# A hybrid SSM and attention block in one kernel: query/key/value projected among the convolution's tiles, z and the gates as half tiles inside the scan and attention

## The reference, cut to what matters

```python
h = rms_norm(x, norm_mix_w)
P = h @ w_in                     # columns [z | xBC | dt | q | k | v | gate_ssm | gate_attn]
u = silu(causal_dwconv(xBC))     # width 4, over 4096 channels
y, state = ssd_scan(xs, softplus(dt + b), -exp(a_log), B, C)   # chunks of 128 tokens; 8 per sample sequence
y = (y + xs * d_skip) * silu(z)
y = y * rsqrt(mean over each of 8 groups (y * y) + eps) * ssm_norm_w
A = y @ w_ssm_out
B = sliding_window_attention(rope(q), rope(k), v, sinks) @ w_attn_out
x = x + (sigmoid(gate_ssm) * A + sigmoid(gate_attn) * B) @ w_out
x = x + peer(rms_norm(x))        # retrieval among 16384 experts, then a final norm
```

## Time and profile before

| | |
|---|---|
| median of 3 runs | 2969.11 us (2968.07 to 2972.53) |
| profiled execution | 2970.44 us around a span of 2968.6 us |
| mean granted clock of TensorE | 0.931 |
| busy share: PE, DVE, ACT, POOL | 93%, 64%, 31%, 23% |
| split on ScalarE (L1021) | 373 x 1.06 us |
| split on GpSimd (L488) | 213 x 2.53 us |

### The profile page before, as it was taken

One profiled execution on the slowest core, in us unless ns is written; L12 is line 12 of the kernel. 1 busy time (PEld: TensorE's weight loads), 2 busy tenths in 40 slices (PEclk: granted clock), 3 DMA queues, 4 the chain that ended last, 5 costly groups with the idle time before them and its releaser, 6 DMA issues.

```text
span 2968.6 us, 46810 instructions
## 1 busy us (share of the span) xinstructions
PE 2768.2 (93%) x15762; PEld 2406.5 (81%) x15762; DVE 1888.6 (64%) x3749; ACT 915.0 (31%) x1527; POOL 683.4 (23%) x345
## 2 busy tenths in 40 slices
PE   6997789997779999989999999999998999999997
PEld 5996668995369999988888888887887888888886
DVE  5998874325620582227799998884667777755554
ACT  2333440044412441123333345553221211211211
POOL 1332000021003324323345423333441111100000
PEclk9998885588869999999999999999999999999999
DMA  3221002321002212312334335457999888866662
GB/s 120 78 78 62 1 0 101 117 96 50 1 27 85 78 64 78 108 66 93 113 132 146 141 149 197 179 191 278 335 342 292 290 289 289 274 196 193 190 196 83
DMA packets 253899, 430.31 MB, mean 145 GB/s; under 512 B 146912, under 2 KB 149600, under 8 KB 252384
## 3 DMA queue, kind: packets, MB, share of 16 engines
q1 hardware_dynamic: 53712, 195.58, 18.7%
q10 hardware_dynamic: 181680, 166.60, 17.0%
q0 software_dynamic: 18432, 67.12, 6.7%
HBM read 349.46 MB, written 81.71 MB: 145 GB/s over the span
## 4 chain that ended last, share of the span: by engine, by line
PE 47%; issue 45%; POOL 6%; DVE 1%; DMA 1%; ACTq 0%; POOLq 0%; ACT 0%; DVEq 0%; SPq 0%
PE ps L955 24%; PE ps L854 19%; POOL wlo L488 6%; PE ps L925 4%; DMA raw<-wt 1%; ACTq L1402 0%; PE ps L534 0%; POOLq L490 0%; DVE y_out L2107 0%; DVE rinv L2105 0%; ACTq L1399 0%; PE ps L905 0%; ACT whi L1021 0%; DVE onehot_i L2004 0%; DVE wlo L2025 0%
## 5 line engine op out<-in xcount | busy, mean ns | idle before, releaser
L488 POOL TENSOR_TENSOR wlo<-raw,whi 128x1024 fp32r<-128x1024 f32 x213 | 539.4, 2533 | 1502.9 <-ACT whi L1021 1502.9
L1021 ACT ACTIVATE whi<-raw 128x1024 fp32r<-128x1024 f32 x373 | 394.9, 1059 | 1478.3 <-PE ps L955 544.7
L854 PE MATMUL ps<-h_hi,whi 128*128 128x512 f32 x1024 | 403.3, 394 | 6.7 <-DVE wlo L2025 4.8
L955 PE MATMUL ps<-act_hi,whi 128*128 128x512 f32 x1024 | 399.4, 390 | 9.1 <-DVE act_lo L1450 9.1
L854 PE MATMUL ps<-h_lo,whi 128*128 128x512 f32 x1024 | 399.8, 390 | 0.0
L854 PE MATMUL ps<-h_hi,wlo 128*128 128x512 f32 x1024 | 399.5, 390 | 0.0
L955 PE MATMUL ps<-act_lo,whi 128*128 128x512 f32 x1024 | 399.2, 390 | 0.0
L955 PE MATMUL ps<-act_hi,wlo 128*128 128x512 f32 x1024 | 399.1, 390 | 0.0
L2025 DVE TENSOR_TENSOR wlo<-raw,whi 128x1024 fp32r<-128x1024 f32 x160 | 196.1, 1225 | 306.3 <-ACT whi L1021 306.3
L525 PE MATMUL ps<-h_hi,whi 128*128 128x288 f32 x1360 | 303.0, 305 | 25.5 <-DVE h_lo L1450 18.9
L525 PE MATMUL ps<-h_hi,wlo 128*128 128x288 f32 x1360 | 296.2, 300 | 0.0
(11 more groups left out here) (282 smaller groups left out, 4068.2 us busy)
## 6 DMA issues: line engine op xcount, KB each, us to landing
raw<-wt SPq DMA_DIRECT2D x245, 512.0 KB, 3.2
raw<-pv SPq DMA_DIRECT2D x128, 512.0 KB, 4.5
activations<-tmp ACTq DMA_DIRECT2D x128, 256.0 KB, 2.0
gates_dense<-g_block ACTq DMA_DIRECT2D x8, 4096.0 KB, 13.1
g_tile<-gates_dense ACTq DMA_DIRECT2D x128, 256.0 KB, 3.6
gelu<-activations ACTq DMA_DIRECT2D x128, 256.0 KB, 4.1
state_s<-s_in ACTq DMA_DIRECT2D x16, 512.0 KB, 4.2
ssm_s<-state_s ACTq DMA_DIRECT2D x16, 512.0 KB, 2.9
```

Source lines behind the costliest of these rows:

```text
L488: pool.tensor_tensor(lo, raw[n.par][:, :], hi.bitcast(F32), ALU.subtract).then_inc(split_ready, 1)
L854: mm = pe.matmul(PS[2 * p.par][:, :], w[slot][:, k, :], x[:, k, 0:SEQ], start=k == 0 and w is whi and x is HH, stop=k == KD - 1 and w is wlo)
L955: mm = pe.matmul(PS[d][:, :], w[s][:, d, :], x[b][:, :], start=first and w is whi and x is ACH, stop=last and w is wlo)
L1021: act.activation(whi[slot][:, :, :].rearrange("p k c -> p (k c)"), raw[slot][:, :], ACT.Copy)\
```

## The change

1. **Order of the tiles.** dt; then six rounds of [two xBC, one of q/k/v] twice (36 tiles); the last 8 of xBC. The 16 tiles of z, 8 attention gates and 8 SSM gates become 32 "side" tiles. Each is two halves of 24 matmuls, always in banks 0 and 1.
2. **Rotary tiles** go, once computed, to `qkv_dram` (12 x 295 KB, on ScalarE's queue) and are loaded again after the scan.
3. **Side tiles.** ScalarE splits the next weights, copies the two banks to one of two buffers and stores it in `side_dram`. Four tiles stand in each chunk of the scan, the sample chunk too: one half after the second and one after the fourth block of transposes, the others in groups 1 to 6. In the prompt chunks a half stands before the group's outputs, in the sample chunk behind them. Two tiles follow the scan, four stand in prompt attention (a half after the transposes of every second unit), two in sample attention (a half behind each pair), four behind the attention's output.
4. **The scan's banks.** Sums move to banks 2 and 3 and the score to bank 6 (in the sample chunk, to free columns of banks 4 and 5); a group's own state uses bank 7 alone and stands behind its outputs. In the sample chunk ScalarE makes the exponentials of group g+2 before it moves the states of g.
5. **Attention's scores** use banks 2 and 3 alone, so scores(u) waits for the masks of u-1.
6. **z** is loaded back in 16 steps between scan and attention, with four buffers: load, Silu, product.
7. **Behind attention**: 8 tiles of the attention's output with a group's sum behind each, the gates loaded at once and Sigmoid in place; the group's root goes into one buffer for all (`RG`), reciprocals are spread; four side tiles; then all of `yn`; then 16 tiles of y's projection, with each SSM gate loaded from `side_dram`.

The number of tiles and of their matmuls is as before. Cut to its core:

```diff
-N_XBC = 1
-N_QKV = N_XBC + CX
-N_ATT = N_QKV + 12
-N_Z = N_ATT + 2 * KD
+N_MIX = 1
+MIXES = 6
+N_XTAIL = N_MIX + 6 * MIXES
+N_SIDE = N_XTAIL + CX - 4 * MIXES
+SIDES = 2 * CI
+SIDES_1, SIDES_2 = 20, 28
+N_AO = N_SIDE + SIDES_2
...
# TensorE
+            def side(n, j, part):
+                if part == 0:
+                    pe.wait_ge(split_ready, n.v + 1)
...
+                        pe.wait_ge(side_used, j)
...
+                for k in range(4 * part, 4 * part + 4):
+                    for w, x in ((whi, HH), (whi, HL), (wlo, HH)):
+                        for h in range(2):
+                            mm = pe.matmul(PS[h][:, 0:HT], w[slot][:, k, :], x[:, k, h * HT:(h + 1) * HT],
...
+                    if q in (1, 3):
+                        fill(q // 2)
...
                     for g in range(NG):
                         back(g)
+                        if 1 <= g <= 6:
+                            fill(g + 1)
                         if g < NG - 2:
                             front(g + 2)
                         new_states(g, 1)
...
                     if g < NG - 1:
                         front(g + 1)
+                    if 1 <= g <= 6:
+                        fill(g + 1)
                     back(g)
...
+            for j in range(SIDES_1, SIDES_1 + 2):
+                for part in range(2):
+                    side(Idx(N_SIDE + j), j, part)
+            pe.wait_ge(qkv_in, 16 * 4)
...
-                if u >= 2:
-                    pe.wait_ge(sc_used, u - 1)
+                if u >= 1:
+                    pe.wait_ge(sc_used, u)
...
                 turn(u)
+                if u % 2 == 0:
+                    j = SIDES_1 + 2 + u // 4
+                    side(Idx(N_SIDE + j), j, u // 2 % 2)
...
+            for m in range(KD):
+                project(Idx(N_AO + m), Idx(P_AO + m), OH, OL)
+                group_sums(m)
+            for j in range(SIDES_2, SIDES):
+                for part in range(2):
+                    side(Idx(N_SIDE2 + j - SIDES_2), j, part)
+            pe.wait_ge(side_used, SIDES)
# ScalarE
+            def side(n, j, k, half):
+                high(plus(n, 2))
...
+                    act.wait_ge(side_out[k], half * 16)
...
+                for h in range(2):
+                    ins = act.activation(SIDE[k][:, h * HT:(h + 1) * HT], PS[h][:, 0:HT], ACT.Copy)
+                ins.then_inc(side_used, 1)
+                act.wait_ge(side_used, j + 1)
+                act.dma_start(dram(side_dram, j), SIDE[k][:, :]).then_inc(side_out[k], 16)
...
+                fill(0)
                 exps(0)
+                if sample:
+                    exps(1)
+                    for g in range(NG):
+                        if g in (2, 4, 6):
+                            fill(g // 2)
+                        if g < NG - 2:
+                            exps(g + 2)
+                        for w in range(2):
+                            move_states(2 * g + w)
+                    return
...
+            for m in range(3):
+                load_z(m)
+            side_at(Idx(N_SIDE + SIDES_1), SIDES_1)
+            for m in range(CI):
+                if m + 3 < CI:
+                    if m:
+                        act.wait_ge(yz_ready, m)
+                    load_z(m + 3)
+                act.wait_ge(z_in[m % 4], 16 * (m // 4 + 1))
+                act.activation(ZB[m % 4][:, :], ZB[m % 4][:, :], ACT.Silu).then_inc(zs_ready, 1)
+                if m == CI // 2:
+                    side_at(Idx(N_SIDE + SIDES_1 + 1), SIDES_1 + 1)
...
+            for m in range(KD):
+                high(Idx(N_AO + m + 2))
+                z_std(m)
+                if m < KD - 1:
+                    z_squares(m + 1)
# VectorE
+            for k in range(2):
+                for j in range(2):
+                    conv(Idx(N_MIX + 3 * k + j), 2 * k + j, j, first=k == 0)
+                rope(Idx(N_MIX + 3 * k + 2), k, k, 0, first=True)
...
+            for m in range(KD):
+                att(m)
+                rinv(m)
+            own.wait()
...
+            for g in range(NG):
+                yn(g)
```

More of the change, by code:

```diff
@@ L81 @@
 SLOTS = P // 2
[L83 to L85 removed]
+P_AO = N_SIDE
+P_SSM = P_AO + KD
+P_OUT = P_SSM + KD
 P_PQ = P_OUT + KD
@@ L234, in build @@
         COS_ = put(misc, "conv_state_sample", [P, CX, SB, 3])
+        side_r = [conv_at, misc[0]]
+        SIDE = [put(side_r, f"side{i}", [P, T]) for i in range(2)]
         DTK = put(misc, "dt_tok", [P, NC, NH])
@@ L262, in build @@
         NA = put(d_r, "neg_a", [P, 1])
+        CS = put(d_r, "cos_sin", [P, 2, T])
+        RS = [put(d_r, f"rope_swap{i}", [P, T]) for i in range(2)]
+        RT = [put(d_r, f"rope_t{i}", [P, T]) for i in range(2)]
         c_r = over(x_r)
@@ new lines, in value @@
+            def value(n, j, k):
+                high(plus(n, 2))
+                act.wait_ge(rope_done, 9 + k)
+                if k == 0:
+                    store_turned(9, 1)
+                halves(RS[k], n, ACT.Copy).then_inc(slot_used[n.par], 1)
+                act.wait_ge(slot_used[n.par], n.half + 1)
+                act.dma_start(dram(qkv_dram, j), RS[k][:, :]).then_inc(q_out[k], 16)
+            for k in range(2):
+                conv_pair(Idx(N_MIX + 3 * k), 2 * k, first=k == 0)
+                swap(Idx(N_MIX + 3 * k + 2), k, k, first=True)
@@ L1119, in ssd @@
                         exps(g + 1)
-                    if sample:
-                        for w in range(2):
-                            move_states(2 * g + w)
+                    if g in (2, 4, 6):
+                        fill(g // 2)
             def load_states(v):
@@ L1158, in _, with load_z @@
-            for k in range(2):
-                swap(Idx(N_QKV + k), k, k, first=True)
-            with act.Fori(1, 5) as i:
-                for k in range(2):
-                    swap(Idx(N_QKV + k, i, 2), i * 2 + k, k)
-            for k in range(2):
-                n = Idx(N_QKV + 10 + k)
-                high(plus(n, 2))
-                halves(VT[k], n, ACT.Copy).then_inc(slot_used[n.par], 1)
+            def load_z(m):
+                act.dma_start(ZB[m % 4][:, :], side_dram[m]).then_inc(z_in[m % 4], 16)
@@ L1228, in _ @@
                     load_cache(4 + 2 * j + k)
+            side_at(Idx(N_SIDE + SIDES_2 - 2), SIDES_2 - 2)
             for j in range(2):
                 attend_pair(1, j)
-            def gate(n, p, buf, tiles, sem=None, value=None):
-                high(plus(n, 2))
-                if sem is not None:
-                    act.wait_ge(sem, value)
-                halves(TMP[buf], p, ACT.Sigmoid).then_inc(slot_used[p.par], 1)
-                for k in range(1, tiles):
-                    high(plus(n, 2 + k))
@@ L1243, in _ @@
-            act.wait_ge(stored, 16 * (6 + 2 * SB))
-            p1 = Idx(P_ATT + 1)
-            for k in range(2):
-                gate(Idx(N_ATT + 2 * k), Idx(P_ATT + 2 * k), k, 2)
-            with act.Fori(1, KD // 2) as i:
-                for k in range(2):
-                    gate(Idx(N_ATT + 2 * k, i, 4), Idx(P_ATT + 2 * k, i, 4), k, 2,
-                         slot_used[p1.par], i * 2 + (k + p1.half - 1))
-            act.wait_ge(slot_used[p1.par], p1.half + KD)
-            def z_tile(g, k, first=False):
-                n = Idx(N_Z + k, g, 2)
-                high(plus(n, 2))
-                if not first:
-                    act.wait_ge(yz_ready, g * 2 + (k - 1))
-                halves(TMP[k], n, ACT.Silu).then_inc(slot_used[n.par], 1)
@@ new lines, in _, with load_gate, ssm_gate @@
+            for m in range(KD):
[3 more added lines that the diff above has]
+                    z_squares(m + 1)
+            for j in range(SIDES_2, SIDES):
+                side_at(Idx(N_SIDE2 + j - SIDES_2), j)
+            def load_gate(m, k):
+                act.dma_start(TMP[k][:, :], dram(side_dram, m + (CI + KD))).then_inc(gate_in[k], 16)
+            def ssm_gate(n, m, k, half, first=False, last=False):
+                act.wait_ge(gate_in[k], half * 16 + 16)
+                act.activation(TMP[k][:, :], TMP[k][:, :], ACT.Sigmoid).then_inc(sgate_ready, 1)
+                for j in range(2):
+                    high(plus(n, 2 + j))
+                if not first:
+                    act.wait_ge(merged, m)
+                if not last:
+                    load_gate(m + 1, 1 - k)
@@ L1546, in ssd @@
                 u0 = c * NG
-                if not start:
+                if start:
+                    for k in range(2):
+                        dve.wait_ge(q_out[k], 16 * 6)
+                else:
                     dve.wait_ge(y_ready, u0)
```

414 lines of the change are left out of this document (224 added, 190 removed).

## The result

The changed kernel took 2980.6 us (median of 7 runs, 2977.7 to 2986.8) against 2969.1 (median of 7, 2967.8 to 2972.5): 1.004 times the time before, 95% interval 1.0029 to 1.0051. It is 11.5 us slower where 9 us faster was forecast; the time lies inside the stated range, the sign is wrong. The profiled span went from 2968.6 to 2978.1 us.

The account below looks back on a forecast made before the run. TensorE was taken to bound most stages, ScalarE and VectorE chains the prompt scan and prompt attention. Terms 67 + 82 + 28 - 38 + 4 + 11 - 163 = -9 us gave 2960 from 2969.1, range 2915 to 2997.

Parts of the forecast that it names:

- Part 2: Four prompt chunks: 16 tiles put in as half tiles, chunks of 62 us against 41.2, +82 us (68 to 92).
- Part 5: Attention: four tiles nearly fit in prompt attention, +4 us (0 to 15); two in sample attention, partly covered, +11 (5 to 20).
- Part 4: Scan's end to first scores: 46.5 us, with z's gates a serial chain on ScalarE, -38 us (-45 to -28).
- Part 1: Convolution stage: 12 query/key/value tiles mixed among 24 convolution tiles, TensorE setting the pace, +67 us (62 to 85).
- Part 6: Attention's end to y's last projection: 28 tiles and eight group sums plus stalls, 219.8 us, -163 us (-170 to -152).
- Part 3: Sample scan: four tiles at 1.2 GHz, state loads issued late behind exponentials, +28 us (-12 to +42).
- third rival: Mixed convolution stage: GpSimd's lock makes VectorE the bound of part 1, +18 us, total +9, 2978 us; 15%.
- first rival: Sample scan: TensorE's clock stays up, -12 us in place of 28, total -49, 2920 us; 17%.
- second rival: Scan and sample attention: half tiles too short, clock rising after 5.8 us serves nothing, total +24, 2993 us; 13%.

Follow-up runs that it names:

- run with early loads: Changed kernel with the store and load of a sample-scan group's first states ahead of the side tile's eviction and the exponentials of group g+2: 2964.4 us.
- combination without the early eviction: Changed kernel with early state loads, half tile behind chunk's outputs with late eviction, z gates loaded first and behind the previous Silu, half tile inside sample-attention pairs: 2923.9 us.
- run with the late eviction: Changed kernel with a half tile behind each prompt chunk's last outputs, its eviction and the first state loads behind the next chunk's first exponentials: 2969.3 us.
- run with the load behind the Silu: Changed kernel with the load of z gate m+3 issued behind the Silu of gate m, not ahead of it: 2975.0 us.

## Why the prediction was wrong

The steps that failed are sizes in the sum, and the two largest lost the sign. Part 2 gave the prompt scan +82 us where it cost +91.2, and part 5 gave sample attention a cover (a wait, and warmth) that hardly came: +11 for +18.8. Parts 4 and 5 (prompt attention) add 7 us. The mechanisms of parts 1, 2 and 6 stood; of those of 3, 4 and 5 a part was missing. By its own steps:

**Part 1 held** (+69.6 for +67). TensorE sets the pace, and the third rival is out: VectorE is busy 26 of 40 us in the mixed stage, not over 95%, and also well under the 17.5 of 19.2 that this part gave it; nothing hung on that.

```profile
120.00:160.00 40.00, 40.00 (x302) 40.00 (x301) 26.40 (x54) 18.87 (x39) 14.47 (x6) 1.00 0.31 105
```

**Part 2 was undersized** (+91.2 for +82), the largest error. Half of the 9.2 us is arithmetic: the parts of a chunk as the text gives them add up to 62.9 us, not 62 (3.6 over four chunks), and 20.8 was rounded down to 20.5 (1.2). The rest is a chunk of 64.1 us, not 62.9. Filled groups take 6.00 us as forecast (outputs at 504.40, 510.39, 516.4, 522.4 us and on). But staging takes 15.6, not 14.8, and the first group to be filled 7.6, since its sums run at half clock behind the wait for the chain; the end, 4.3 for 5.3, gave 1 back.

```profile
498.86 1.91 PE L667 MATMUL ps<-consts_sb,da_chunk 128*128 128x128 f32 x8
```

Later the same eight sums cover 1.05 us. Half a microsecond here is 2 us in the sum.

**Part 3 had the right mechanism** (+25.5 for +28): the load behind the exponentials, shown by the run that moves it. That the size fits too is partly luck. The step named only the wait, 4.2 us a group (its own 13.4 and 15.0 against 9.6 would be 4.6); in the trace TensorE's idle time in the stage grew by 12.8 us and its busy time by 11.8, where the step had nearly all as waiting. The run with early loads gives 7 us to the waits and the other 11 to the clock that outputs lose behind one.

**Part 4 missed the loads** (-34.8 for -38). The chain runs in 1.88 us steps, somewhat better than the 2.05 forecast, but ScalarE waited 6.35 us for its first load, issued behind those of q, k, v and the masks, which the step did not count though the change puts them on that queue. Its own terms, put end to end (9, 2.5, 32.6, 2.7, 2), are 48.8 us, not 46.5; that alone would be -36.

**Part 5 named the wrong cover.** Prompt attention (+7.9 for +4): 1.4 us are the first scores at half clock, 2.2 the shared banks, the rest the half tiles, of which the first, ahead of the third unit's scores, costs most. Sample attention (+18.8 for +11) is the step that failed most in proportion. It took "1 of a wait and some 1.6 of warmth" off each half tile's 5.4; the four halves last 5.0 to 5.8 us, 21.5 together, and the stage grew by 18.8, so some 0.7 of the 2.6 came. The wait that a half tile could cover lies between a pair's scores and its transposes, not behind its values, as the run that moves it shows. Pairs take 15.9 to 18.0 us against 12.3, and in the third pair GpSimd's split holds an instruction of VectorE's on a single column in the chain (timelines of both):

```profile
1015.46 1.97 DVE L1895 SCALAR_TENSOR_TENSOR att_small<-att_small,params_sb 128x1 f32<-128x1 f32 x1
...
1015.07 2.34 POOL L508 TENSOR_TENSOR wlo<-raw,whi 128x1024 fp32r<-128x1024 f32 x1 [37.68 <-ACT whi L1085]
```

That is the hold of the earlier trace rows again, which the Trainium skill ("SBUF — State Buffer", "Who interferes with whom") describes; the trace agrees, with 1.97 us for an instruction that reads two SBUF operands and takes 0.16 elsewhere in the stage.

**Part 6 was better than forecast** (-170.4 for -163): of the 9 us for y's normalization 1.1 came (6.3 in the second profile of the same kernel, so part of this is luck), of the 5.4 for the gates' load 2.2.

The first rival (clock up through the sample scan) did not happen: outputs run at 0.50 in the changed kernel. Its mechanism, work that can't lift the clock may hold it, is real, as the run with early loads shows, but it lasted for some microseconds only. At 724 us of that run the clock falls between instructions without a gap. The Trainium skill ("TensorE: Matmul & The Clock Gate", "Why this matters for your kernels") has it lost by idle gaps; the prediction found the trace against the first half of that rule, and here it is against the second too. The second rival's condition was met in places (halves of 5.8 and 5.7 us in sample attention, at 1042 and 1008 us, with a granted clock of 0.54 and 0.56), its 24 us were not.

The sign was lost because the forecast was a difference of 9 us between terms that add up to some 200 on either side, of which two were short by 9.2 and 7.8. The chance of slower, 0.32, was fair; the 0.50 for faster was not earned by terms known to 10%. That every term kept its sign is owed to the mechanisms; that the time stayed inside a range 82 us wide says little. And the gain that the change could bring was there: the same tiles in the same stages, with the seams mended, give 2918.6 us, 2.1% less than the changed kernel and 1.8% less than the one before.

## What to carry to other kernels

Work moved into another stage is free only while the engine would have waited there; look up that wait in the trace and put the work into it, not behind it, and let the short matmuls that gain from a lifted clock follow directly. Of an engine that issues transfers, ask for each inserted step what stands behind it on that queue (here state loads, a store, an exponential): the order of a few lines on ScalarE was worth 18.3 us in the sample scan, and an eviction ahead of a store 7.1. Where a forecast is the small rest of large terms, the seams (first, last and cold instances of a loop) decide its sign, and they are read one by one.

## What the runs showed that was not expected

Matmuls of 8 columns held a clock that the same matmuls did not lift anywhere in the kernel before (full clock in 744.0 to 746.8 of the run with early loads, 0.50 through the sample scan in the earlier trace rows), and lost it without a gap at 724.

The chunks depend on the granted clock too: with the same code there, the profile of the combination without the early eviction has chunks of 59.5, 58.0, 58.0 and 57.7 us, 8 less in all than the run with the late eviction; in all four its first filled group takes 6.0 us, where the other run has 7.6 in three, which is 5 of the 8.

The mixed stage has two paces at a granted clock of 1.00 with TensorE busy throughout: 302 matmuls in 40 us in most profiles, 310 in two (the run with the load behind the Silu, and the combination without the early eviction), where the stage ended at 340.8 and 342.4 us, not 347 to 349. TensorE between 160 and 200 us in the changed kernel and in the former of the two:

```profile
160.00:200.00 40.00, 40.00 (x302) 1.00 0.30 93
```

```profile
160.00:200.00 40.00, 40.00 (x310) 1.00 0.33 107
```

It makes 6 to 8 us, and likely part of the 9 us over which the changed kernel's runs scatter. What sets it stays open. So does why the sample scan gained 6.8 us by the eviction ahead of the split, and a part of the scatter behind attention (1.1 to 11.2 us of waiting for y).
